# Half of the experts' weight loads issued through ScalarE's DMA queue

## The chip, the cores and the metric

The kernel runs on one core of one Trainium2 chip. The metric is device time in microseconds of one execution; lower is better. PE is TensorE, DVE is VectorE, ACT is ScalarE, POOL is GpSimd and SP is SyncE, the engine that here does nothing but wait and issue DMAs.

## The reference

Two transformer blocks in a row on one sequence of 256 tokens with 1024 channels, all in float32. The first has attention and an MLP; the second has an mLSTM branch, a differential attention branch and, last, a mixture of 16 experts in which each expert chooses its 32 tokens:

```python
def expert_choice_ffn(h, w_router, w_gate, w_up, w_down):
    aff = softmax(einsum('bsd,de->bse', h, w_router))
    g, idx = lax.top_k(aff.transpose(0, 2, 1), cap)          # cap = 32 tokens for each of 16 experts
    xe = h[bidx, idx]
    hid = silu(einsum('becd,edf->becf', xe, w_gate)) * einsum('becd,edf->becf', xe, w_up)
    ye = einsum('becf,efd->becd', hid, w_down) * g[..., None]
    return zeros_like(h).at[bidx, idx].add(ye)
# second block: x = x + expert_choice_ffn(rms_norm(x)); then a final rms_norm(x) * norm_f_g
```

Each expert has three matrices, gate and up of 1024 x 2048 and down of 2048 x 1024, 8 MB each. The experts' weights are 402.7 MB in all, and each byte is used once.

## The kernel before

The experts' stage is the second part of the program, from about 550 us on. The weights of an expert come in six **units** of 4 MB: unit u = 6e + kind, where kinds 0 and 1 are the two halves of the gate matrix of expert e, 2 and 3 those of the up matrix, 4 and 5 those of the down matrix. There are 96 units, 0 to 95. A unit is a load of 128 partitions by 32 KB, contiguous in memory for each partition. It goes into one of five buffers of `expert_ring`. Unit 5 has a place of its own, so that from unit 11 on, unit u takes the buffer that unit u - 5 has left.

PE works through the units in order, 32 matmuls each (L1255 for gate and up, L1294 for down), and counts `pairs_used` up twice in each unit, so that `pairs_used >= 2u + 2` says that unit u is used. Between kinds 3 and 4 of an expert DVE forms the product of silu and up (L1957), PE transposes it (L669) and DVE copies it back (L1963); after every fourth expert's kind 3 PE also gathers the tokens of the next four experts (L1199). After kind 5 ACT copies the expert's result `ye` and PE scatters it into the sum in PSUM (L1303).

Before the change all unit loads are issued by SP, in order, in one loop (L642). For each unit it waits until the unit that holds the buffer is used and then issues the DMA:

```python
if n >= BUFFERS:
    sp.wait_ge(pairs_used, 2 * unit_of(n - BUFFERS) + (1 if halved(u) else 2))
src = gate_up[kind // 2][e, kind % 2] if kind < 4 else down[e, kind - 4]
if not halved(u):
    sp.dma_start(expert_ring[:, FILL[b], :], src).then_inc(unit_loaded[b], 16)
    continue
```

A few units are loaded in pieces (`halved`): the first ones, 6 and 7, and the last, 95, which comes as 2 MB, 1 MB and two times 512 KB (L645, L649). PE waits on `unit_loaded` of the buffer before the first matmul of a unit.

ACT has three instructions for each expert: the silu after kind 1 (L2327), the copy `selx` of the scatter matrix (L2332, after kind 3), and the copy of `ye` after kind 5 (L2334). At expert 12 it also issues the load of the final gain row `gfinal`, 4 KB spread to 128 partitions (L2330), which is used only after the last expert. After the last expert come the final norm on ACT (L2338) and DVE (L1970) and the stores.

Of the kernel before, what the change touches and what calls it, by code (L numbers as in the profile page):

```python
# [37 lines left out]
P = 128  # L38
# [11 lines left out]
EXPERTS = 16  # L50
# [17 lines left out]
BUFFERS = 5  # L68
FILL = (3, 4, 0, 1, 2)
UNITS_EACH = 6  # L70
# [77 lines left out]
def build_program(nc, A, out, bias_scratch):  # L148
    with ExitStack() as ctx:
# [3 lines left out]
        def sems(text):  # L153
            return [ctx.enter_context(nc.semaphore(n)) for n in text.split()]
# [15 lines left out]
        expert_ring = nc.alloc_sbuf_tensor_at("expert_ring", [P, BUFFERS, UNIT], F32, offset=ring_at)  # L170
# [49 lines left out]
        def view(at, *shape):  # L220
# [79 lines left out]
        unit_loaded = [ctx.enter_context(nc.semaphore(f"unit_loaded{i}")) for i in range(BUFFERS)]  # L300
# [35 lines left out]
        pairs_used, selx_turned, selx_ready, silu_set, hid_set, hid_turned, hidT_set, ye_set, scattered_first, scattered = sems(  # L336
            "pairs_used selx_turned selx_ready silu_set hid_set hid_turned hidT_set ye_set scattered_first scattered")
# [31 lines left out]
        def used(g):  # L369

            if g == G_WOUT0:
                return g + 1 + N_ADA12
            return g + 1 - (G_ADA12 <= g < G_ADA12 + N_ADA12)
# [9 lines left out]
        def split_done(eng, g):  # L383

            eng.wait_ge(slot_split, 2 * (SPLIT.index(g) + 1))
# [28 lines left out]
        def fill_of(u):  # L414

            return u - (u > APART)

        def unit_of(n):

            return n + (n >= APART)  # L420

        def fills(u):

            return [unit_of(n) for n in range(fill_of(u) % BUFFERS, fill_of(u) + 1, BUFFERS)]
# [5 lines left out]
        def halved(u):  # L430

            return u in (1, 2, 3, APART + 1, APART + 2, EXPERTS * UNITS_EACH - 1)

        def second_of(u):

            return 16 * sum(2 if n in (1, 2) else 1 for n in fills(u) if halved(n))

        def everywhere(row, n):

            return bass.AP(row.tensor, row.offset, [[0, P], [1, n]])  # L440
# [84 lines left out]
        @block.sync  # L525
        def _(sp):
            sp.dma_start(xres[:, :, :], A["x"][0].rearrange("(t p) d -> p t d", p=P)).then_inc(x_in, 16)
            down = A["w_down_e_2"][0].rearrange("e (q p c) n -> e q p (c n)", q=2, p=P)
            gate_up = [A[n][0].rearrange("e (p h k) n -> e h p (k n)", p=P, h=2) for n in ("w_gate_e_2", "w_up_e_2")]

            def load_gain(which, k):

# [56 lines left out]
            for u in range(1, EXPERTS * UNITS_EACH):  # L589
                e, kind, n = u // UNITS_EACH, u % UNITS_EACH, fill_of(u)  # L590
                b = n % BUFFERS
                if u == 1:
                    def early(u, at, to, sem):

                        b = fill_of(u) % BUFFERS
                        kind = u % UNITS_EACH
                        sp.dma_start(expert_ring[:, FILL[b], at * SLOT:to * SLOT],
                                     gate_up[kind // 2][u // UNITS_EACH, kind % 2][:, at * SLOT:to * SLOT])\
                            .then_inc(sem[b], 16)

                    sp.wait_ge(unit_out, 2 * MH)
                    early(1, 0, 2, unit_loaded)
                    split_done(sp, G_UP + 3)
                    early(2, 0, 2, unit_loaded)
                    sp.wait_ge(mixed, 2)
                    early(1, 2, 3, second_loaded)
                    split_done(sp, G_WOUT2)
                    early(2, 2, 3, second_loaded)
                    sp.wait_ge(mixed, 4)
                    early(1, 3, 4, second_loaded)  # L610
                    sp.dma_start(ahead_y, down[0, 1][:, 4 * D:6 * D]).then_inc(ahead_loaded, 16)
                    split_done(sp, G_WOUT2 + 1)
                    early(2, 3, 4, second_loaded)
                    split_done(sp, G_WOUT2 + 2)
                    early(3, 0, 1, unit_loaded)
                    split_done(sp, G_WOUT2 + 3)
                    early(3, 1, 2, unit_loaded)
                    sp.wait_ge(slots_used, used(G_WOUT2 + 2))
                    early(3, 2, 4, second_loaded)
                    sp.wait_ge(slots_used, PRELUDE)  # L620
                if u <= 3:
                    continue
                if u == APART:
                    sp.wait_ge(logit16, 2)
                    sp.dma_start(ahead_x, down[0, 1][:, 6 * D:7 * D]).then_inc(ahead_x_loaded, 16)
                    continue
                if u == APART + 3:
                    sp.wait_ge(rank_cols, 1)
                    sp.dma_start(ahead_c, down[0, 1][:, 7 * D:8 * D]).then_inc(ahead_c_loaded, 16)
                if u == APART + 1:  # L630
                    sp.wait_ge(slots_used, PRELUDE + 1)
                    early(u, 0, 1, unit_loaded)
                    sp.wait_ge(pairs_used, 1)
                    early(u, 1, 2, unit_loaded)
                    sp.wait_ge(pairs_used, 2)
                    early(u, 2, 4, second_loaded)
                    continue
                if n >= BUFFERS:
                    sp.wait_ge(pairs_used, 2 * unit_of(n - BUFFERS) + (1 if halved(u) else 2))
                src = gate_up[kind // 2][e, kind % 2] if kind < 4 else down[e, kind - 4]  # L640
                if not halved(u):
                    sp.dma_start(expert_ring[:, FILL[b], :], src).then_inc(unit_loaded[b], 16)  # L642
                    continue
                if u == EXPERTS * UNITS_EACH - 1:
                    sp.dma_start(expert_ring[:, FILL[b], 0:4 * D], src[:, 0:4 * D]).then_inc(unit_loaded[b], 16)  # L645
                    sp.wait_ge(pairs_used, 2 * unit_of(n - BUFFERS) + 2)
                    for sem, first, last in zip(tail_loaded, (4, 6, 7), (6, 7, 8)):
                        part = slice(first * D, last * D)
                        sp.dma_start(expert_ring[:, FILL[b], part], src[:, part]).then_inc(sem, 16)  # L649
                    continue  # L650
                for half, sem in enumerate((unit_loaded[b], second_loaded[b])):
                    part = slice(half * UNIT // 2, (half + 1) * UNIT // 2)
                    if half == 1:
                        sp.wait_ge(pairs_used, 2 * unit_of(n - BUFFERS) + 2)
                    sp.dma_start(expert_ring[:, FILL[b], part], src[:, part]).then_inc(sem, 16)
            for t in range(NT):
                for half in range(2):
                    c = slice(512 * half, 512 * (half + 1))
# [1318 lines left out]
        def _(act):  # L1977
# [35 lines left out]
            def expect(function):  # L2013

                N.activation(foreseen[:, :], eps[:, :], function)
# [109 lines left out]
            for half in range(2):  # L2125
                for i in range(half * MLP_HALF, (half + 1) * MLP_HALF):
                    if g_w1(i) not in RAW:
                        act.wait_ge(slots_used, used(g_w1(i)))
                        for m in range(2):
                            c = A_B1 + 2 * i + m  # L2130
# [7 lines left out]
                    c = 2 * (i % MLP_HALF)  # L2138
# [24 lines left out]
            for i in range(N_MIX2):  # L2163
                if i < N_MIX2 - 1:
                    round_slot(act, G_MIX2 + i + 2)
                if i in range(4, 4 + 8):
                    c = i - 4
# [8 lines left out]
                if i < 4:  # L2176
                    dst, src = zpad[:, 2 * i:2 * i + 2, 2:2 + S], turned_
                elif i == 5:
                    dst, src = vo[:, 1, 0:MW], PS[:, i % 4, :]
                elif i < 10:  # L2180
                    dst, src = dqk[:, 2 * (i - 6):2 * (i - 6) + 2, :], turned_
                elif i == 11:
                    dst, src = dv[:, 1, :], PS[:, i % 4, :]
                else:
                    dst, src = vo[:, 1, MW:2 * MW], PS[:, i % 4, :]
# [39 lines left out]
            for u in range(2 * MH + 1):  # L2225
# [6 lines left out]
                if u == MH + 2:  # L2232
                    act.wait_ge(factors2_set, 1)
                    for t in range(NT):
                        for h in range(MH):
                            n, w = 8 * t + h, work[:, t, h * P:(h + 1) * P]
# [30 lines left out]
            for t in range(NT):  # L2267
                for u in range(MH, 2 * MH):
                    n, w = 8 * t + u, work[:, t, u * P:(u + 1) * P]
# [50 lines left out]
            normalise(1, slice(4, KD))  # L2320
            act.wait_ge(exp16, 1)
            expect(ACT.Silu)
            for e in range(EXPERTS):
                act.wait_ge(pairs_used, 2 * (UNITS_EACH * e + 2))
                if e == 0:
                    act.wait_ge(seeded, 2 * NT)
                N.activation(silu[:, :], PS[:, 0, :], ACT.Silu).then_inc(silu_set, 1)  # L2327
                if e == EXPERTS - GROUP:
                    act.wait_ge(gathered, 2 * EXPERTS // GROUP + 3)
                    act.dma_start(gfinal, everywhere(A["norm_f_g_2"], D)).then_inc(gfinal_in, 16)  # L2330
                act.wait_ge(selx_turned, e + 1)
                N.activation(selx[:, :], PS[:, 0, 0:S], ACT.Copy).then_inc(selx_ready, 1)  # L2332
                act.wait_ge(pairs_used, 2 * (UNITS_EACH * e + 6))
                N.activation(ye[:, :], PS[:, 3, :], ACT.Copy).then_inc(ye_set, 1)  # L2334
            expect(ACT.Sqrt)
# [86 lines left out]
```

## Time and profile before

| | us |
|---|---|
| median of 3 runs | 1452.87 (1452.32 to 1454.32) |
| the profiled execution | 1452.38 |
| its span | 1450.6 |
| PE busy | 1060.3 (73%) |
| DVE busy | 425.8 (29%) |
| ACT busy | 346.2 (24%) |
| POOL busy | 85.8 (6%) |

The span is what the hardware profiler saw from the first to the last instruction; the execution's own time is a little longer. Shares are of the span. The DMA queues moved 514.50 MB at a mean of 355 GB/s; q1 is SP's hardware queue, q10 is ACT's, q0 is POOL's, and q8 and q14 fetch instructions.

### The profile page before, as it was taken

How to read it: one execution, taken by the hardware profiler on the slowest of the kernel's cores; microseconds unless marked ns; L12 is line 12 of the kernel's file. 1: busy time of each engine (PE TensorE's matmuls, PEld its weight loads, DVE VectorE, ACT ScalarE, POOL GpSimd, SP SyncE). 2: the span in 40 equal slices, each digit the busy share in tenths (PEclk: the TensorE clock that was granted, in tenths of full speed). 3: DMA queues.
4: the chain of work that ended last, by engine and by line, in shares of the span. 5: the costliest groups of instructions: out<-in, count | busy, mean ns of one | idle time of the engine just before them, and what ended most of it. 6: DMA issues, size and time to landing. Idle time of an engine off the chain costs nothing.

```text
span 1450.6 us, 15820 instructions
## 1 busy us (share of the span) xinstructions
PE 1060.3 (73%) x6734; PEld 599.1 (41%) x6734; DVE 425.8 (29%) x767; ACT 346.2 (24%) x600; POOL 85.8 (6%) x60
## 2 busy tenths in 40 slices
PE   6999999999999999766665565565545565655655
PEld 3866888888989985211211111121111121111111
DVE  3577776756979863000000000000000000000001
ACT  3566654636555942000000000000000000000001
POOL 1420059000000000000000000000000000000000
PEclk9999999999999999988888887788788878788788
DMA  9996468554564689999999999999999999999996
GB/s 362 338 376 205 147 230 262 191 186 146 175 232 125 261 342 418 431 431 430 428 432 432 432 431 430 432 431 430 429 431 432 433 433 428 431 429 431 433 432 279
DMA packets 83144, 514.50 MB, mean 355 GB/s; under 512 B 6659, under 2 KB 49134, under 8 KB 67330
## 3 DMA queue, kind: packets, MB, share of 16 engines
q1 hardware_dynamic: 82360, 512.68, 87.4%
q8 instruction: 53, 0.87, 0.3%
q10 hardware_dynamic: 490, 0.61, 0.1%
q0 software_dynamic: 224, 0.20, 0.0%
q14 instruction: 17, 0.14, 0.0%
HBM read 512.27 MB, written 1.07 MB: 354 GB/s over the span
## 4 chain that ended last, share of the span: by engine, by line
DMA 56%; PE 33%; DVE 7%; ACT 2%; issue 1%; SPq 1%; POOL 0%; DVEq 0%; ACTq 0%
DMA expert_ring<-in_w_up_e 20%; DMA expert_ring<-in_w_gate_e 18%; DMA expert_ring<-in_w_down_e 15%; PE PS L1255 6%; PE PS L675 5%; PE PS L677 5%; PE PS L676 5%; PE PS L722 4%; PE PS L724 2%; DVE wR L403 2%; PE PS L1294 2%; DMA ring<-in_w_in 1%; PE PS L749 1%; DMA ring<-in_w_ada 1%; ACT wR L393 1%
## 5 line engine op out<-in xcount | busy, mean ns | idle before, releaser
L1255 PE MATMUL PS<-expert_ring,xeT 128*32 128x512 f32 x2048 | 309.7, 761 | 225.9 <-DMA expert_ring<-in_w_up_e 124.0
L1255 PEld LDWEIGHTS PS<-expert_ring,xeT 128*32 128x32 f32 x2048 | 74.3, 135 | 458.1 <-issue 207.7
L1957 DVE TENSOR_TENSOR expert_rows<-expert_rows,PS 128x512 f32<-128x512 f32 x16 | 11.0, 687 | 805.6 <-PE PS L1255 805.6
L1294 PE MATMUL PS<-expert_ring,expert_rows 128*32 128x512 f32 x992 | 155.4, 777 | 103.7 <-DMA expert_ring<-in_w_down_e 101.4
L403 DVE TENSOR_TENSOR wR<-ring,wR 128x1024 fp32r<-128x1024 f32 x144 | 177.8, 1276 | 55.3 <-ACT wR L393 55.0
L393 ACT ACTIVATE wR<-ring 128x1024 fp32r<-128x1024 f32 x144 | 144.5, 1053 | 112.0 <-PE PS L677 110.8
L1294 PEld LDWEIGHTS PS<-expert_ring,expert_rows 128*32 128x32 f32 x992 | 38.7, 137 | 208.9 <-issue 119.5
L722 PE MATMUL PS<-hR,wR 128*128 128x512 f32 x320 | 112.2, 396 | 1.7 <-DVE wR L403 1.6
L724 PE MATMUL PS<-hR,wR 128*128 128x256 f32 x320 | 89.1, 278 | 0.0
L2332 ACT ACTIVATE selx<-PS 128x256 f32<-128x256 f32 x16 | 6.1, 384 | 322.4 <-PE PS L669 322.4
L675 PE MATMUL PS<-hR,wR 128*128 128x256 f32 x280 | 80.2, 286 | 0.8 <-DVE wR L403 0.8
L677 PE MATMUL PS<-hR,wR 128*128 128x256 f32 x280 | 79.2, 283 | 0.0
L676 PE MATMUL PS<-hR,wR 128*128 128x256 f32 x280 | 79.2, 283 | 0.0
L2327 ACT ACTIVATE expert_rows<-PS 128x512 f32<-128x512 f32 x16 | 9.6, 597 | 283.7 <-PE PS L1255 283.7
L2334 ACT ACTIVATE expert_rows<-PS 128x512 f32<-128x512 f32 x16 | 9.6, 597 | 257.0 <-PE PS L1294 257.0
L722 PEld LDWEIGHTS PS<-hR,wR 128*128 128x128 f32 x320 | 60.0, 188 | 16.5 <-issue 2.4
L724 PEld LDWEIGHTS PS<-hR,wR 128*128 128x128 f32 x320 | 60.2, 188 | 0.1
L675 PE MATMUL PS<-wR,hR 128*128 128x512 f32 (+1 forms) x144 | 55.7, 386 | 1.7 <-DVE wR L403 1.4
L677 PE MATMUL PS<-wR,hR 128*128 128x512 f32 (+1 forms) x144 | 54.3, 377 | 0.0
L676 PE MATMUL PS<-wR,hR 128*128 128x512 f32 (+1 forms) x144 | 54.3, 377 | 0.0
L675 PEld LDWEIGHTS PS<-hR,wR 128*128 128x128 f32 x280 | 53.7, 192 | 1.1 <-issue 1.0
L676 PEld LDWEIGHTS PS<-hR,wR 128*128 128x128 f32 x280 | 53.7, 192 | 0.0
(317 smaller groups left out, 1281.9 us busy)
## 6 DMA issues: line engine op xcount, KB each, us to landing
expert_ring<-in_w_down_e SPq DMA_DIRECT2D x30, 4096.0 KB, 44.2
expert_ring<-in_w_up_e SPq DMA_DIRECT2D x30, 4096.0 KB, 43.1
expert_ring<-in_w_gate_e SPq DMA_DIRECT2D x29, 4096.0 KB, 43.2
ring<-in_w SPq DMA_DIRECT2D x32, 1024.0 KB, 6.1
ring<-in_w_in SPq DMA_DIRECT2D x31, 1024.0 KB, 5.7
ring<-in_w_ada SPq DMA_DIRECT2D x16, 1024.0 KB, 12.8
ring<-in_w_out SPq DMA_DIRECT2D x8, 1024.0 KB, 10.6
expert_ring<-in_w_gate_e SPq DMA_DIRECT2D x4, 2048.0 KB, 12.4
```

The lines of the kernel that those rows point to most:

```text
L393: nc.scalar.activation(halves(g, 0)[:, piece], slot(g)[:, piece], ACT.Copy).then_inc(slot_rounded, 1)
L403: by.tensor_tensor(halves(g, 1)[:, piece], slot(g)[:, piece], halves(g, 0)[:, piece], ALU.subtract)\
L675: nc.tensor.matmul(o, first[0], second[0], start=start, stop=False, skip_group_check=onto)
L676: nc.tensor.matmul(o, first[0], second[1], start=False, stop=False, skip_group_check=onto)
L677: return nc.tensor.matmul(o, first[1], second[0], start=False, stop=stop, skip_group_check=onto)
L722: nc.tensor.matmul(o.rearrange("p (a s) -> p a s", a=2), w[0][:, k, cols], hR[:, :, k, :], start=(k == 0), stop=False, skip_group_check=True)
L724: mm = nc.tensor.matmul(o[:, 0:S], w[1][:, k, cols], hR[:, 0, k, :], start=False, stop=(k == KD - 1), skip_group_check=True)
L749: mm = nc.tensor.matmul(PS[:, bank, m * S + t * P:m * S + (t + 1) * P], k8(g)[:, k, m * P:(m + 1) * P], hT[:, k, t * P:(t + 1) * P], start ...
L1255: mm = nc.tensor.matmul(PS[32 * j:32 * j + 32, kind // 2, :], xeT[:, e // GROUP % 2, k, own], w[:, j // 2, j % 2, :, :], start=(k == 0), s ...
L1294: mm = nc.tensor.matmul(PS[32 * at:32 * at + 32, 3, :], hidT[:, c % 4, 2 * q + c // 4, :], w[c][:, 512 * half:512 * (half + 1)], start=(q ...
L1957: V.tensor_tensor(hid[:, :], silu[:, :], PS[:, 1, :], ALU.mult).then_inc(hid_set, 1)
L2327: N.activation(silu[:, :], PS[:, 0, :], ACT.Silu).then_inc(silu_set, 1)
```

## The change

From unit 13 on, every odd unit but the last (13, 15, ... 93, 41 loads) is issued by ACT. SP skips these units. ACT waits for the use of unit u before it issues unit u + 5, and this is put at three places of its loop over the experts: ahead of the silu, ahead of the copy of selx and ahead of the copy of ye. Source, destination, size and semaphore of each load stay as they were, and so does the unit whose use it waits for.

```diff
+        def by_act(u):
+
+            return u > 2 * UNITS_EACH and u % 2 == 1 and u < EXPERTS * UNITS_EACH - 1
+
+        down = A["w_down_e_2"][0].rearrange("e (q p c) n -> e q p (c n)", q=2, p=P)
+        gate_up = [A[n][0].rearrange("e (p h k) n -> e h p (k n)", p=P, h=2) for n in ("w_gate_e_2", "w_up_e_2")]
+
+        def unit_source(u):
+
+            e, kind = u // UNITS_EACH, u % UNITS_EACH
+            return gate_up[kind // 2][e, kind % 2] if kind < 4 else down[e, kind - 4]
+
...
+                if by_act(u):
+                    continue
                 if n >= BUFFERS:
                     sp.wait_ge(pairs_used, 2 * unit_of(n - BUFFERS) + (1 if halved(u) else 2))
-                src = gate_up[kind // 2][e, kind % 2] if kind < 4 else down[e, kind - 4]
+                src = unit_source(u)
...
+
+            def load_behind(u):
+
+                if u + 5 < EXPERTS * UNITS_EACH and by_act(u + 5):
+                    act.wait_ge(pairs_used, 2 * u + 2)
+                    b = fill_of(u + 5) % BUFFERS
+                    act.dma_start(expert_ring[:, FILL[b], :], unit_source(u + 5)).then_inc(unit_loaded[b], 16)
+
             for e in range(EXPERTS):
+                load_behind(UNITS_EACH * e)
                 act.wait_ge(pairs_used, 2 * (UNITS_EACH * e + 2))
...
+                load_behind(UNITS_EACH * e + 2)
                 act.wait_ge(selx_turned, e + 1)
                 N.activation(selx[:, :], PS[:, 0, 0:S], ACT.Copy).then_inc(selx_ready, 1)
+                load_behind(UNITS_EACH * e + 4)
                 act.wait_ge(pairs_used, 2 * (UNITS_EACH * e + 6))
```

## Rows read from the trace of the kernel before

**Rows 1.** The page: its head, and the chain that ended last by engine.

```profile
span 1450.6 us, 15820 instructions
...
DMA 56%; PE 33%; DVE 7%; ACT 2%; issue 1%; SPq 1%; POOL 0%; DVEq 0%; ACTq 0%
```

**Rows 2.** Windows: stretch, us, busy by engine (instructions), PE clock, DMA share, GB/s.

```profile
650.00:700.00 50.00, 29.91 (x186) 8.18 (x182) 1.77 (x4) 0.98 (x2) 0.00 (x0) 0.81 1.01 433
...
1300.00:1400.00 100.00, 55.28 (x348) 15.11 (x348) 3.54 (x8) 2.56 (x5) 0.00 (x0) 0.84 1.00 430
```

**Rows 3.** Waits: engine and line, whom for, us in total, times, longest.

```profile
ACT selx L2332 <- PE PS L669: 322.4, 16, 24.8
ACT expert_rows L2327 <- PE PS L1255: 283.7, 16, 19.9
ACT expert_rows L2334 <- PE PS L1294: 257.0, 16, 19.8
...
SPq L642 <- PE PS L1255: 491.8, 53, 12.3
```

**Rows 4.** Timeline: start, length, instruction, count [idle before, releaser].

```profile
588.07 10.51 PE L1255 MATMUL PS<-expert_ring,xeT 128*32 128x512 f32 x96
...
599.07 3.64 PE L1255 MATMUL PS<-expert_ring,xeT 128*32 128x512 f32 x32 [0.49 <-DMA expert_ring<-in_w_up_e]
...
1223.92 5.49 PE L1255 MATMUL PS<-expert_ring,xeT 128*32 128x512 f32 x32 [6.08 <-DMA expert_ring<-in_w_gate_e]
1229.48 0.37 ACTq L2330 DMA_DIRECT2D ybuf<-in_norm_f_g  x1
1233.69 5.34 PE L1255 MATMUL PS<-expert_ring,xeT 128*32 128x512 f32 x32 [4.28 <-DMA expert_ring<-in_w_up_e]
1244.47 5.45 PE L1255 MATMUL PS<-expert_ring,xeT 128*32 128x512 f32 x32 [5.45 <-DMA expert_ring<-in_w_up_e]
1254.28 5.34 PE L1294 MATMUL PS<-expert_ring,expert_rows 128*32 128x512 f32 x32 [2.57 <-DMA expert_ring<-in_w_down_e]
1263.89 5.98 PE L1294 MATMUL PS<-expert_ring,expert_rows 128*32 128x512 f32 x32 [4.27 <-DMA expert_ring<-in_w_down_e]
...
1302.73 5.34 PE L1255 MATMUL PS<-expert_ring,xeT 128*32 128x512 f32 x32 [4.64 <-DMA expert_ring<-in_w_up_e]
```

**Rows 5.** DMA, 600 to 1400 us: queues (packets, MB, share of engines), issues (median us to landing).

```profile
q1 hardware_dynamic: 11806, 343.94, 100.0%
...
q10 hardware_dynamic: 144, 0.52, 0.2%
...
expert_ring<-in_w_up_e SPq DMA_DIRECT2D x28, 4096.0 KB, 43.1
```

**Rows 6.** DMA queues, 1229.5 to 1233.5 us, then 1233.5 to 1244.5.

```profile
q10 hardware_dynamic: 7, 0.03, 1.8%
...
q1 hardware_dynamic: 145, 4.23, 89.0%
q10 hardware_dynamic: 137, 0.50, 11.1%
```

**Rows 7.** Timeline of the end.

```profile
1376.04 0.33 SPq L642 DMA_DIRECT2D expert_ring<-in_w_up_e  x1
...
1420.82 6.02 PE L1255 MATMUL PS<-expert_ring,xeT 128*32 128x512 f32 x32 [4.37 <-DMA expert_ring<-in_w_up_e]
...
1428.44 0.69 DVE L1963 COPY expert_rows<-PS 128x512 f32<-128x512 f32 x1 [0.84 <-PE PS L669]
...
1430.62 3.64 PE L1294 MATMUL PS<-expert_ring,expert_rows 128*32 128x512 f32 x32 [2.00 <-DMA expert_ring<-in_w_down_e]
...
1440.37 1.05 PE L1294 MATMUL PS<-expert_ring,expert_rows 128*32 128x512 f32 x4 [0.18 <-DMA expert_ring<-in_w_down_e]
1441.47 0.60 ACT L2334 ACTIVATE expert_rows<-PS 128x512 f32<-128x512 f32 x1 [12.42 <-PE PS L1294]
```

**Rows 8.** Timeline of a gather and the unit behind it.

```profile
1191.08 3.84 PE L1199 MATMUL PS<-sel,work 128*128 128x128 f32 x32
...
1197.24 3.64 PE L1294 MATMUL PS<-expert_ring,expert_rows 128*32 128x512 f32 x32 [0.56 <-DVE expert_rows L1963]
```

More of the change, by code:

```diff
@@ L527, in _ @@
             sp.dma_start(xres[:, :, :], A["x"][0].rearrange("(t p) d -> p t d", p=P)).then_inc(x_in, 16)
-            down = A["w_down_e_2"][0].rearrange("e (q p c) n -> e q p (c n)", q=2, p=P)
-            gate_up = [A[n][0].rearrange("e (p h k) n -> e h p (k n)", p=P, h=2) for n in ("w_gate_e_2", "w_up_e_2")]
             def load_gain(which, k):
```

## The prediction

> **What bounds the kernel now.** I read the page's head and its chain of work first [rows 1]. The profiled execution took 1452.38 us, 1.78 more than its span. DMA is the largest share of the chain (56%), nearly all of it the experts' weights. The windows by stage [rows 2] say where: from 650 to 1400 us the DMA engines' busy share is 1.00 or 1.01 at 430 to 433 GB/s, while PE is busy 55 to 61 us of each 100. PE sits idle before its units until one lands [rows 4]. So the experts' stage is set by bytes over rate and ends when the last unit has landed; what follows is a short tail. In the waits [rows 3] SP, too, waits for little but used buffers, and ACT waits some twenty us before each instruction of this stage.
>
> Landings come 9.71 us apart: unit 77 is taken up at 1263.89 and unit 81 at 1302.73, four loads in 38.84 [rows 4]. Between 600 and 1400 us q1 moved 343.94 MB in 11806 packets [rows 5]. That is 82.0 loads of 4.194 MB and 144 packets a load, 9 for each of 16 engines. The 128 rows of 32 KB give 8 large ones each, and the ninth is small. 9.71 / 8 = 1.21 us per large packet. Five buffers, each refilled as soon as it is used, keep 4.4 loads outstanding (43.1 us to landing over 9.71).
>
> **The change, part by part.** 41 loads (units 13, 15, ... 93) leave SP's queue. On SP that removes 41 issues of 0.33 us [rows 7], hidden there: over four loads were queued in front of each. On ACT it adds 41 waits and 41 issues, which I price at the 0.37 us of ACT's own DMA issue in this stage [rows 4], 15 us in all. Behind them on ACT stand the silu, the copy of selx and the copy of ye. Each of these waits for a unit after the one that the load ahead of it waits for, at least 3.6 us later, so an issue is over when they are released. The cover is ACT's idle time before those three (284, 322 and 257 us [rows 3]); without it 15 us would be the cost. I take 0. Each moved load waits for the same unit's use as before.
>
> *The rate with two queues.* No stretch has two streams of large packets. The nearest is gfinal, 512 KB on ACT's queue (q10) beside SP's loads. Between 1233.5 and 1244.5 us q10 moved 137 packets and q1 145 [rows 6]: one for one, whatever their size. From unit 73 to 77, with gfinal between them, the landings took 39.97 us [rows 4]; four loads alone take 38.84, so gfinal cost 1.13 us, where 0.52 MB at 431 GB/s would be 1.22. From 73 to 76 (30.36 less 3 x 9.71) it cost 1.23, from 74 to 75 (10.78 less 9.71) 1.07. So 16 changes of queue on each engine cost between -0.15 and +0.01 us. In the new kernel some 85 loads of 8 packets alternate, 680 changes: -6.4 to +0.4 us. I take 0, since the engines' busy share leaves nothing that a second queue could fill.
>
> The Trainium skill (DMA: Bandwidth & Descriptors, "Issuing engines are not separate DMA queues") speaks against any gain: DMAs of all issuing engines run on the same 16 and interleave, so spreading them saves only issue time. By it alone the sum would be 0 and the time 1452.9; on the rate, the rows of gfinal agree. It says nothing of what the interleaving does to the order of landing, which is worked out next from rows.
>
> *The order of landing.* While both queues hold work each load takes 16 turns, 2 x 9.71 = 19.4 us, and an odd and an even one are under way together. PE then meets two units at once: about 5.9 us for the first after a long idle (5.49 and 6.02 [rows 4, 7]), 3.64 for the second. From issue to first packets I take 4 us, as gfinal's (issued 1229.48 [rows 4], 7 of its 144 packets before 1233.5 [rows 6]). Units 6 to 8 end at 598.6 and 9 is there at 599.1 [rows 4]. So 13 is issued at 598.6, starts at 602.6 and lands at 622, before its turn. Beside it 10 has 3 packets at 1.21 us and 5 at 2.43: it lands at 615, 11 at 631. 15, issued when 10 is used (620.7), runs from 624.7 to 644; 17 is not issued until 12 is used, near 653.5, and starts at 657.5. In that gap SP's queue has all engines and catches up: 14 lands at 657, then 16 and 17 both near 677. From there on ACT's next load is ready in time (even landing + 5.9 + 4 is less than 19.4), and units 2k and 2k + 1 land within a us or two of each other. The DMA engines never run dry: a pair costs PE 5.9 + 3.64, plus 2.4 for the transposes and 3.8 more where a gather falls in [rows 7, 8], under 16 of 19.4 us. So the last byte lands when it did.
>
> Then expert 12: gfinal now stands in ACT's queue behind unit 77. It takes 8 turns with 4 KB packets, while SP's queue takes 8 turns with 32 KB, a whole load. From there the odd loads are one place later: 79 lands with 80, not with 78, and so on to 93 with 94. That is the step that costs. At the end now, 93 is taken up at 1420.82, 94 at 1430.62, the last piece of 95 at 1440.37, and PE ends 1.05 later [rows 7]. If 93 lands X us before the last piece, PE still has to do after it: 6.0 (unit 93) + 2.4 (product, transposes, copy: 1426.84 to 1429.2) + 3.64 (unit 94) + 3.64 (unit 95, all there by then) = 15.7 us; the last two at full clock, as the unit behind a gather ran (3.64 after 0.56 idle [rows 8]). The end moves by 15.7 - X - 1.05 where that is positive. 93 landing exactly with 94 gives X = 9.75 and +4.9. One us earlier gives X = 10.3 (what remains of 94 then gets all engines) and +4.35. I take that. Bounds: 93 some 10 us ahead of 94 gives X = 14.7 and 0; 93 five us behind 94, while 95 runs beside it, gives X = 7.3 and +7.4.
>
> Sum: issues 0, rate 0, tail +4.35, the epilogue (from 1441.47 on [rows 7]) unchanged. The profiled execution would take 1456.7, and the median of the runs, now 0.5 above it, 1457.2.
>
> **Rivals.**
> *No change (1452.9, up to 1455).* The odd loads keep a lead of 5 us or more over their even partners. If a load's first packet comes 1.5 us after its issue and PE's first unit of a pair is short, 17 and 19 start sooner, the lead outlives gfinal, and 93 lands 14 us or more before the end. For it: bytes and rate. Against: gfinal's 4 us and the eight turns lost to it.
> *A larger loss (1461 to 1468).* Two interleaved streams of large packets cost the engines something that gfinal, one 4 KB row read 128 times, could not show: 1% of 850 us is 8.5, to 1461. Or ACT's queue is served less than one for one: then 93 would land last, X near 0, +14.6, 1467.5. Against both: 145 to 137, and -0.15 to +0.01.
> *Faster (1446.5 to 1450).* If each of 680 changes of queue gives back the 0.009 us of the lower bound, -6.4 with a tail of 0 gives 1446.5; beside a tail of 4.35 it would have to be more than 7.3 to be told from no change. Against: a busy share of 1.00 already, and landings that repeat to 0.1 us.
> *That the change does nothing* is excluded: ACT's DMAs have a queue of their own, q10, beside SP's q1 [rows 5].
>
> **How the numbers follow.** 0.2% is 2.9 us, about what these runs can tell from no change. Tail as forecast (+0 to +7.4, likeliest +4.35): 0.55, of which 0.08 lies under +2.9. No change: 0.28. Larger loss: 0.11. Faster: 0.06. So slower 0.47 + 0.11 = 0.58, same 0.08 + 0.28 = 0.36, faster 0.06. The range leaves out most of the larger loss and of the faster case, and holds the others: 1451.0 to 1461.5; the forecast's own is 1453 to 1460.
>
> **What would show it.** Right: a DMA share of 1.00 and 430 to 433 GB/s in the same windows; q10 with about 172 MB; odd and even units landing together every 19.4 us and PE in bursts of two; odd loads one place later after gfinal; unit 93 within 12 us of the last piece of 95, and PE without a wait for that piece. Wrong: 93 landing 15 us or more before the end (no tail), fewer GB/s (two streams cost something), stretches with a DMA share under 1.00 before 1430 us (starved engines), or PE waiting for ACT.

## The result, and the profile after

The changed kernel takes 1457.98 us (median of 5 runs, 1457.05 to 1459.0) against 1452.71 for the kernel before beside it (1451.88 to 1454.32): a ratio of 1.0038, 95% interval 1.0026 to 1.0049. Run once more (e8 below) it gave 1.0028, 1.0017 to 1.0040. The profiled execution took 1457.91 us, with a span of 1456.1. Three executions, one of the kernel before and one each of e2 and e3 below, took 1647.58 to 3781.58 us and are left out of all ratios; e2's was its profiled one, so e5 is the same kernel again, for its trace.

First the windows of the changed kernel, with the columns of [rows 2]:

```profile
650.00:700.00 50.00, 27.28 (x214) 8.05 (x210) 1.77 (x4) 1.58 (x3) 0.00 (x0) 0.84 1.01 433
...
1300.00:1400.00 100.00, 53.86 (x362) 14.24 (x352) 3.54 (x8) 3.15 (x6) 0.00 (x0) 0.76 1.00 429
1400.00:1440.00 40.00, 21.15 (x142) 5.39 (x142) 1.38 (x2) 0.98 (x2) 0.00 (x0) 0.79 0.93 395
1440.00:1446.00 6.00, 6.00 (x60) 1.81 (x59) 0.00 (x0) 0.00 (x0) 0.00 (x0) 1.00 0.03 14
```

The DMA engines are as full as before and move the same GB/s. What is new is the last row: from 1440 to 1446 us next to nothing is left to load (14 GB/s), and PE is busy all six us. In the kernel before PE ended 1.05 us after it took up the last piece.

The DMA queues of the changed kernel from 600 to 1400 us, as in [rows 5]:

```profile
q1 hardware_dynamic: 6102, 177.93, 51.7%
q10 hardware_dynamic: 5833, 166.50, 48.4%
...
expert_ring<-in_w_gate_e ACTq DMA_DIRECT2D x14, 4096.0 KB, 32.5
expert_ring<-in_w_up_e SPq DMA_DIRECT2D x14, 4096.0 KB, 49.5
...
ybuf<-in_norm_f_g ACTq DMA_DIRECT2D x1, 512.0 KB, 39.4
```

The two queues share the bytes about evenly. Where every load took 43 to 45 us from issue to landing, ACT's now take some 32 and SP's some 49. Over the whole execution q10 moved 172.58 MB. gfinal takes 39.4 instead of 15.1, since it waits for ACT's loads ahead of it.

Then PE's timeline in the changed kernel (L1267 and L1306 are L1255 and L1294 of before), as in [rows 4, 7]. A row of x64 is two units without a wait between them; where the product and its transposes lie between the two units of a pair, as between 81 and 82, they are two rows:

```profile
589.32 10.51 PE L1267 MATMUL PS<-expert_ring,xeT 128*32 128x512 f32 x96
600.44 3.64 PE L1267 MATMUL PS<-expert_ring,xeT 128*32 128x512 f32 x32 [0.62 <-DMA expert_ring<-in_w_up_e]
...
617.53 5.39 PE L1306 MATMUL PS<-expert_ring,expert_rows 128*32 128x512 f32 x32 [11.67 <-DMA expert_ring<-in_w_down_e]
633.23 6.07 PE L1306 MATMUL PS<-expert_ring,expert_rows 128*32 128x512 f32 x32 [10.31 <-DMA expert_ring<-in_w_down_e]
...
649.01 8.44 PE L1267 MATMUL PS<-expert_ring,xeT 128*32 128x512 f32 x64 [6.91 <-DMA expert_ring<-in_w_gate_e]
659.95 7.08 PE L1267 MATMUL PS<-expert_ring,xeT 128*32 128x512 f32 x64 [2.49 <-DMA expert_ring<-in_w_up_e]
...
679.46 8.58 PE L1306 MATMUL PS<-expert_ring,expert_rows 128*32 128x512 f32 x64 [10.66 <-DMA expert_ring<-in_w_down_e]
...
1264.25 9.72 PE L1306 MATMUL PS<-expert_ring,expert_rows 128*32 128x512 f32 x64 [7.94 <-DMA expert_ring<-in_w_down_e]
...
1276.69 3.64 PE L1267 MATMUL PS<-expert_ring,xeT 128*32 128x512 f32 x32
1295.53 9.45 PE L1267 MATMUL PS<-expert_ring,xeT 128*32 128x512 f32 x64 [15.19 <-DMA expert_ring<-in_w_gate_e]
1314.96 6.54 PE L1267 MATMUL PS<-expert_ring,xeT 128*32 128x512 f32 x32 [9.98 <-DMA expert_ring<-in_w_up_e]
...
1430.93 6.58 PE L1267 MATMUL PS<-expert_ring,xeT 128*32 128x512 f32 x32 [9.64 <-DMA expert_ring<-in_w_up_e]
...
1439.86 7.07 PE L1306 MATMUL PS<-expert_ring,expert_rows 128*32 128x512 f32 x64 [0.56 <-DVE expert_rows L1975]
```

Read it by units. 10 and 11 come late, 16 us apart. 12 and 13 are done together at 649.01, 16 and 17 at 679.46, and so on in pairs of an even unit with the odd one above it, up to 76 with 77 at 1264.25. Then 78 is done alone (1276.69), and PE waits 15.19 us for 79, which is done with 80 (1295.53). From there each pair is odd first (81, with 82 behind the transposes, at 1314.96), and 93 starts at 1430.93. Behind it PE never waits for a weight again: 94 and 95 are one row of 64 matmuls, released by DVE's copy, not by a load.

The start of the experts' stage differs between executions, here by 1.25 us. So I also measure from the start of unit 6 (588.07 and 589.32) to PE's end of unit 95 (1440.37 + 1.05 = 1441.42, and 1439.86 + 7.07 = 1446.93): 853.35 us before, 857.61 after, +4.26.

### The profile page after: what moved, and what is told of

Its sections match the earlier page's. It is cut to its first block, busy times and chain, and to the rows that moved or that the text cites. A ratio compares the mean times of both kernels' runs of the same rounds, so it can differ in the third digit from the quotient of the medians.

```text
span 1456.1 us, 15820 instructions
## 1 busy us (share of the span) xinstructions
PE 1023.5 (70%) x6734; PEld 595.0 (41%) x6734; DVE 425.5 (29%) x767; ACT 346.1 (24%) x600; POOL 86.0 (6%) x60
## 3 DMA queue, kind: packets, MB, share of 16 engines
q10 hardware_dynamic: 6394, 172.58, 27.6%
## 4 chain that ended last, share of the span: by engine, by line
DMA 47%; PE 39%; DVE 7%; ACT 2%; another core or an unknown queue 2%; issue 2%; SPq 1%; POOL 0%; DVEq 0%; ACTq 0%
DMA expert_ring<-in_w_up_e 30%; DMA expert_ring<-in_w_down_e 13%; PE PS L1267 8%; PE PS L687 5%; PE PS L689 5%; PE PS L688 5%; PE PS L734 4%; PE PS L1306 4%; DMA expert_ring<-in_w_gate_e 3%; PE PS L736 2%; DVE wR L403 2%; DMA ring<-in_w_ada 2%; PE PS L681 1%; SPq L564 1%
## 5 line engine op out<-in xcount | busy, mean ns | idle before, releaser
L1267 PE MATMUL PS<-expert_ring,xeT 128*32 128x512 f32 x2048 | 288.2, 724 | 247.6 <-DMA expert_ring<-in_w_up_e 132.5
L1267 PEld LDWEIGHTS PS<-expert_ring,xeT 128*32 128x32 f32 x2048 | 71.3, 130 | 460.5 <-issue 212.4
L1306 PE MATMUL PS<-expert_ring,expert_rows 128*32 128x512 f32 x992 | 139.4, 722 | 124.1 <-DMA expert_ring<-in_w_down_e 121.8
L1306 PEld LDWEIGHTS PS<-expert_ring,expert_rows 128*32 128x32 f32 x992 | 37.3, 130 | 215.5 <-issue 185.3
```

Source lines behind the costliest of these rows:

```text
L1267: mm = nc.tensor.matmul(PS[32 * j:32 * j + 32, kind // 2, :], xeT[:, e // GROUP % 2, k, own], w[:, j // 2, j % 2, :, :], start=(k == 0), s ...
L1306: mm = nc.tensor.matmul(PS[32 * at:32 * at + 32, 3, :], hidT[:, c % 4, 2 * q + c // 4, :], w[c][:, 512 * half:512 * (half + 1)], start=(q ...
```

## The experiments

Three explanations had to be told apart. **Order of landing**: gfinal's packets cost ACT's queue eight turns (a turn is one packet of one queue on one DMA engine), so the odd loads fall one place back, 93 lands with 94, and PE is left with 93, 94 and 95 behind the last loads. **Pairs**: that units land two at a time costs by itself, through PE's bursts. **Two queues**: their alternation or ACT's issues cost rate. All times are ratios to the kernel before, run beside each; "stage" is the stretch defined above.

| | ratio, 95% interval | stage, us | against before |
|---|---|---|---|
| before | 1 | 853.35 | |
| changed kernel | 1.0038, 1.0026 to 1.0049 | 857.61 | +4.26 |
| e1, gfinal on SP | 0.9997, 0.9988 to 1.0005 | 853.34 | -0.01 |
| e2 and e5, unit 93 on SP | 1.0000, 0.9991 to 1.0009 (e2) | 853.21 (e5) | -0.14 |
| e3, quarter of gfinal | 1.0019, 1.0009 to 1.0028 | 855.55 | +2.20 |
| e4, even units on ACT | 1.0028, 1.0017 to 1.0039 | 858.53 | +5.18 |
| e6, odd units from 79 | 1.0003, 0.9993 to 1.0012 | 853.29 | -0.06 |
| e7, gfinal in four | 1.0036, 1.0022 to 1.0050 | 858.48 | +5.13 |
| e8, changed kernel again | 1.0028, 1.0017 to 1.0040 | 857.77 | +4.42 |

**e1, gfinal on SP's queue.** All 41 loads stay on ACT.

```diff
+                if u == 78:
+                    sp.wait_ge(pairs_used, 2 * (UNITS_EACH * 12 + 2))
+                    sp.wait_ge(gathered, 2 * EXPERTS // GROUP + 3)
+                    sp.dma_start(gfinal, everywhere(A["norm_f_g_2"], D)).then_inc(gfinal_in, 16)
...
-                if e == EXPERTS - GROUP:
-                    act.wait_ge(gathered, 2 * EXPERTS // GROUP + 3)
-                    act.dma_start(gfinal, everywhere(A["norm_f_g_2"], D)).then_inc(gfinal_in, 16)
```

> The changed kernel, with the load of gfinal issued by SP ahead of unit 78 instead of by ACT behind unit 77. Order-of-landing theory: ACT's queue no longer loses eight turns, so the odd loads stay beside the even load one below them; 93 lands with 92, about 19 us before the last piece of 95, PE waits for that piece again, and the time is that of the kernel before, 1452.7, within 2 us. Rival, pairs cost by themselves (bursts of PE at a lower clock, whichever pairs they are): the loss of about 5 us stays, 1458. Rival, two queues or ACT's issues cost rate: it stays too, and shows as fewer GB/s before 1430 us.

Median 1451.91 us of 11 runs; before 1452.5. The whole loss is gone. Its timeline on PE, around gfinal and at the end:

```profile
1265.36 9.19 PE L1310 MATMUL PS<-expert_ring,expert_rows 128*32 128x512 f32 x64 [9.01 <-DMA expert_ring<-in_w_down_e]
...
1294.43 16.88 PE L1271 MATMUL PS<-expert_ring,xeT 128*32 128x512 f32 x128 [17.08 <-DMA expert_ring<-in_w_gate_e]
...
1402.73 8.78 PE L1271 MATMUL PS<-expert_ring,xeT 128*32 128x512 f32 x64 [6.67 <-DMA expert_ring<-in_w_gate_e]
1422.15 9.30 PE L1271 MATMUL PS<-expert_ring,xeT 128*32 128x512 f32 x64 [10.65 <-DMA expert_ring<-in_w_up_e]
...
1433.81 6.47 PE L1310 MATMUL PS<-expert_ring,expert_rows 128*32 128x512 f32 x56 [0.57 <-DVE expert_rows L1979]
1440.46 1.05 PE L1310 MATMUL PS<-expert_ring,expert_rows 128*32 128x512 f32 x4 [0.18 <-DMA expert_ring<-in_w_down_e]
1441.69 1.05 PE L1310 MATMUL PS<-expert_ring,expert_rows 128*32 128x512 f32 x4 [0.18 <-DMA expert_ring<-in_w_down_e]
```

92 and 93 are one row at 1422.15, and the last two pieces are each waited for again. Pairs and two queues are here in full, with 167.68 MB on q10 between 600 and 1400 us, and cost nothing: both rivals fall.

One thing I had not expected: gfinal held up SP's queue here. 78 is taken up 29.07 us after 76 (1265.36 to 1294.43), not 19.4, and 78 to 81 are one row of 128 matmuls. But this place was won back: from 1295 to 1300 us q10 moved nothing and q1 ran at a share of 1.01, and behind it the pairs are even with odd again, down to 92 with 93. So a place lost to gfinal does not always stay lost; it did in ACT's queue.

**e2 and e5, unit 93 on SP's queue.** gfinal stays on ACT.

```diff
-            return u > 2 * UNITS_EACH and u % 2 == 1 and u < EXPERTS * UNITS_EACH - 1
+            return u > 2 * UNITS_EACH and u % 2 == 1 and u < EXPERTS * UNITS_EACH - 3
```

> The changed kernel, with unit 93 given back to SP (ACT has 13 to 91); gfinal stays on ACT. Order-of-landing theory: odd loads still fall one place back at expert 12, and 91 lands with 92, but from there SP's queue holds 93, 94 and 95 in order with all engines to itself; 93 lands about 19 us before the last piece, no backlog, 1452.7 within 2 us. Both rivals (cost of pairs, cost of two queues): 40 of 41 moved loads are still moved, so at least 4.5 of the 5 us stay, 1457.5 or more.

> The same kernel as e2_unit93_on_sync, for its trace. Order-of-landing theory: 79 lands with 80 and 91 with 92 as in the changed kernel (odd loads one place back), then 93 alone about 19 us and 94 about 10 us before the last piece of 95, and PE waits for that piece. Rival, that giving 93 back undid the shift itself: 91 lands with 90.

e2: median 1453.06 of 11 runs, ratio 1.0000. One load of 41 carries the loss. e5, a single execution of 1454.28 us, shows how, in PE's timeline:

```profile
1276.92 3.64 PE L1267 MATMUL PS<-expert_ring,xeT 128*32 128x512 f32 x32 [0.67 <-DMA expert_ring<-in_w_gate_e]
1296.25 9.88 PE L1267 MATMUL PS<-expert_ring,xeT 128*32 128x512 f32 x64 [15.69 <-DMA expert_ring<-in_w_gate_e]
...
1413.17 13.19 PE L1267 MATMUL PS<-expert_ring,xeT 128*32 128x512 f32 x96 [7.56 <-DMA expert_ring<-in_w_gate_e]
...
1432.52 10.80 PE L1306 MATMUL PS<-expert_ring,expert_rows 128*32 128x512 f32 x64 [4.38 <-DMA expert_ring<-in_w_down_e]
```

The shift at 79 is there as in the changed kernel. But 91, 92 and 93 are one row of 96 matmuls ending at 1426.36, and PE waits 4.38 us for 94. The wait for the last piece of 95 that I expected is not there: 94 and 95 are one row, 10.80 us long at a granted clock that was 0.50 from 1432 to 1438 us, yet it ends in time. So the shift costs nothing until it meets the end.

**e3, a quarter of gfinal.** Only 256 of the gain row's 1024 columns are loaded, so the output's other columns are scaled by what lay there.

```diff
-                    act.dma_start(gfinal, everywhere(A["norm_f_g_2"], D)).then_inc(gfinal_in, 16)
+                    act.dma_start(gfinal[:, 0:D // 4], everywhere(A["norm_f_g_2"], D // 4)).then_inc(gfinal_in, 16)
```

> The changed kernel, with gfinal loaded for its first 256 of 1024 columns only (three quarters of the final gain row are left unloaded, so the final scaling reads other values there): 1 KB rows in place of 4 KB, 128 of them as before. Theory that turns are lost, one for each packet whatever its size: eight turns as before, odd loads one place back from 79 on, 93 within 12 us of the last piece, 1457 (0.9 us less than now for the 0.39 MB not moved). Theory that what counts is the bytes or the time of the transfer in ACT's queue: the shift is a quarter, the odd loads keep near the even load below them, 93 lands 17 us or more before the last piece and the loss is gone, 1452 to 1453.

Median 1455.8, 1.2 us under what I expected, but clear of no change. PE's timeline:

```profile
1276.23 3.64 PE L1267 MATMUL PS<-expert_ring,xeT 128*32 128x512 f32 x32
1293.85 8.42 PE L1267 MATMUL PS<-expert_ring,xeT 128*32 128x512 f32 x64 [13.97 <-DMA expert_ring<-in_w_gate_e]
...
1429.26 5.55 PE L1267 MATMUL PS<-expert_ring,xeT 128*32 128x512 f32 x32 [9.00 <-DMA expert_ring<-in_w_up_e]
```

The shift is whole: 78 alone, 79 with 80. With a quarter of the bytes it would have been a quarter if bytes or time counted; the number of packets was unchanged. The stage is 2.06 us shorter than the changed kernel's. 1.03 of it is unit 93 itself (5.55 for 6.58 us), 1.03 its earlier start (840.58 for 841.61 us from the start of unit 6), for which the missing bytes would give 0.9 by my estimate. The first part does not come of the edit: e8, with all of gfinal, has unit 93 at 5.42 us.

**e4, the even units on ACT**, the odd ones on SP, and gfinal on SP.

```diff
-            return u > 2 * UNITS_EACH and u % 2 == 1 and u < EXPERTS * UNITS_EACH - 1
+            return u > 2 * UNITS_EACH and u % 2 == 0 and u < EXPERTS * UNITS_EACH - 1
...
-                load_behind(UNITS_EACH * e)
...
+                load_behind(UNITS_EACH * e + 1)
...
-                load_behind(UNITS_EACH * e + 2)
+                load_behind(UNITS_EACH * e + 3)
...
-                load_behind(UNITS_EACH * e + 4)
+                load_behind(UNITS_EACH * e + 5)
```

> The mirror of the change: the even units 14 to 94 on ACT (issued behind the use of the odd units), the odd ones on SP, and gfinal on SP ahead of unit 79. Order-of-landing theory: without any turn lost the pairs are 13 with 14, 15 with 16, up to 93 with 94, since ACT's load lands with the SP load one below it; so the tail comes back with no part of gfinal: 93 within 12 us of the last piece, +4 to +6 over before, 1457 to 1459. Theory that gfinal's place in ACT's queue costs in some other way than by the pairing: 1452.7 within 2.

Median 1456.63. The loss is back with gfinal out of ACT's queue. By its edit alone this run does not separate the parity from gfinal, since gfinal stands again in the queue of the odd units. PE's and SP's timelines do, with the end behind them:

```profile
1234.42 9.42 PE L1271 MATMUL PS<-expert_ring,xeT 128*32 128x512 f32 x64 [7.45 <-DMA expert_ring<-in_w_gate_e]
1240.46 0.33 SPq L651 DMA_DIRECT2D ybuf<-in_norm_f_g  x1
...
1303.55 8.99 PE L1271 MATMUL PS<-expert_ring,xeT 128*32 128x512 f32 x64 [18.23 <-DMA expert_ring<-in_w_gate_e]
...
1431.51 6.42 PE L1271 MATMUL PS<-expert_ring,xeT 128*32 128x512 f32 x32 [9.49 <-DMA expert_ring<-in_w_up_e]
...
1440.29 7.07 PE L1310 MATMUL PS<-expert_ring,expert_rows 128*32 128x512 f32 x64 [0.56 <-DVE expert_rows L1979]
```

73 and 74 are a pair, odd first, before gfinal is issued; 79 comes late (gfinal is ahead of it in SP's queue), but with 80, so the pairs are the same behind gfinal as ahead of it. The parity makes them, without gfinal. The end is the picture of the changed kernel: 93 late, and 94 and 95 one row behind it.

**e6, the odd units from 79 on.** ACT issues eight loads, and gfinal comes ahead of them.

```diff
-            return u > 2 * UNITS_EACH and u % 2 == 1 and u < EXPERTS * UNITS_EACH - 1
+            return u > 13 * UNITS_EACH and u % 2 == 1 and u < EXPERTS * UNITS_EACH - 1
```

> The change made for the odd units from 79 to 93 only (8 loads); gfinal stays on ACT, where it is now ahead of all of ACT's unit loads. Order-of-landing theory: gfinal's eight turns are over before unit 79 stands in the queue or cost it at most a short wait, 79 gets ahead as unit 13 did, the pairs settle as 2k with 2k + 1 within some units, 93 lands with 92, about 19 us before the last piece: 1452.5 within 2 us. Theory that any odd load on ACT next to gfinal or at the end costs: +4 to +5, 1457.

Median 1452.12, ratio 1.0003. At the end PE's timeline has 92 and 93 as one row:

```profile
1420.83 10.05 PE L1267 MATMUL PS<-expert_ring,xeT 128*32 128x512 f32 x64 [9.90 <-DMA expert_ring<-in_w_up_e]
```

So neither gfinal on ACT nor unit 93 on ACT costs anything alone. With the odd units on ACT, it takes gfinal among ACT's loads.

**e7, gfinal in four transfers** of 256 columns at the same place: the same bytes, four times the packets.

```diff
-                    act.dma_start(gfinal, everywhere(A["norm_f_g_2"], D)).then_inc(gfinal_in, 16)
+                    for c in range(0, D, D // 4):
+                        row = A["norm_f_g_2"]
+                        part = bass.AP(row.tensor, row.offset + c, [[0, P], [1, D // 4]])
+                        act.dma_start(gfinal[:, c:c + D // 4], part).then_inc(gfinal_in, 16)
...
-            dve.wait_ge(gfinal_in, 16)
+            dve.wait_ge(gfinal_in, 16 * 4)
```

> The changed kernel, with gfinal loaded by ACT in four transfers of 256 columns, so the same bytes in four times the packets (32 for each engine in place of 8), at the same place. Turn theory: while ACT's queue spends 32 turns on small packets, SP's queue sends out all it has (some 20 packets for each engine), so 79 lands some 30 us after 78, not 20 as in the changed kernel; PE and SP then wait for 79, and the pairs settle again as 79 with 80 and so on (SP cannot run further ahead than its buffers), so the end is as in the changed kernel: 1457 to 1460. Byte theory: 79 comes 20 us after 78 as in the changed kernel.

PE's timeline around 79:

```profile
1275.99 3.64 PE L1267 MATMUL PS<-expert_ring,xeT 128*32 128x512 f32 x32
1303.50 8.59 PE L1267 MATMUL PS<-expert_ring,xeT 128*32 128x512 f32 x64 [23.87 <-DMA expert_ring<-in_w_gate_e]
```

and its windows while PE waits there:

```profile
1280.00:1290.00 10.00, 0.00 (x0) 0.00 (x0) 0.00 (x0) 0.00 (x0) 0.00 (x0) 0.64 1.01 429
1290.00:1300.00 10.00, 0.00 (x0) 0.00 (x0) 0.00 (x0) 0.00 (x0) 0.00 (x0) 0.50 1.00 431
```

79 starts 714.87 us after unit 6, where the changed kernel has 706.21 and 706.96 (e8): some 8 us later for the same bytes. From 78 to 79 it is 27.5 us (30 expected), where the changed kernel has 18.8 and 20.3 (e8). A cost for each transfer, four in place of one, would fit that too, but the queues from 1265 to 1285 us show the turns:

```profile
q1 hardware_dynamic: 284, 8.26, 95.9%
q10 hardware_dynamic: 284, 0.26, 3.8%
```

Packet for packet, with 8.26 MB for one queue and 0.26 MB for the other. Turns are what is lost. Even a wait of 23.87 us costs nothing there that these runs can tell, since the DMA engines stay full. The pairs then settle as in the changed kernel, and so does the time (1457.52).

**e8, the changed kernel again.**

> The changed kernel itself, once more, beside the other one on the same chip: 1.003 to 1.0045 of the kernel before by either theory. It gives the spread of the start of the experts' stage, 1.25 us later in the changed kernel's trace than in that of before: if the change caused that, its trace shows it again and the loss is 5.3 us; if not, the loss is the tail's, 4.2.

Median 1456.79 of 6 runs. Its PE timeline:

```profile
586.11 10.51 PE L1267 MATMUL PS<-expert_ring,xeT 128*32 128x512 f32 x96
...
1429.03 5.42 PE L1267 MATMUL PS<-expert_ring,xeT 128*32 128x512 f32 x32 [9.10 <-DMA expert_ring<-in_w_up_e]
```

Here the stage starts 1.96 us earlier than in the kernel before, not 1.25 later, so the start belongs to the execution and not to the change. From unit 6 on the loss is 4.42 us.

## Why the prediction was right, point by point

- **ACT's issues, 0 us.** Right. e1 has all 41 at a ratio of 0.9997.
- **The rate, 0 us (bounds -6.4 to +0.4).** Right. 431 GB/s and a DMA share of 1.00 with two full streams, and e1 again bounds it: its interval, -1.7 to +0.7 us, holds everything the two queues can do.
- **How the pairs form.** Predicted for 10, 11, 12, 14 and 16: 615, 631, 648, 657 and 677; with the 1.25 us of the later start the trace has them at 617.5, 633.2, 649.0, 659.95 and 679.5, so they come between 0.2 us before and 1.7 us after the forecast. The 4 us from issue to first packets, which went into these, is in the trace: ACT issues unit 13's load at 599.89, q10 moves nothing before 603.3, and 11 packets of it start in the next us.
- **gfinal moves the odd loads one place back.** Right: 79 with 80. That it is the number of turns, not bytes, rested on 137 against 145 packets before; e3 (fewer bytes, same shift) and e7 (same bytes, larger shift, 284 packets against 284) show it. That the place stays lost down to 93 I took without a reason: it held here, but e1 won its place back.
- **The tail, +4.35 us.** The trace has +4.26, and +4.42 in e8. By its terms, measured from the start of unit 6: the last byte came when it did before (the DMA share is 0.00 from 851.9 us on before, from 852.2 or sooner after), the last piece was taken up at 852.30 before, and 93 at 841.61, so X is 10.7 (10.3 predicted). Behind it came 6.58 + 2.35 + 7.07 = 16.0 us (15.7 predicted). In e8 93 was taken up at 842.92, so X is 9.4, and 14.85 us came behind it. So each term moves by a us between executions of the same kernel, in these two the same way, and their difference hardly did: that the sum hit within 0.1 us is in part luck. The runs' 1.0038 is 5.5 us and e8's 1.0028 is 4.1; 4.35 (1.0030) lies in both intervals.
- **The rivals.** No change: e1, e2 and e6 have its time, so it was close, one 512 KB transfer or one unit away. A larger loss from two streams or from an unevenly served queue: refuted by the rate and by e1. Faster: refuted by the same.

The time (1457.98) lies 0.8 us from the forecast of 1457.2; against the kernel before beside it the runs have +5.3 us, where +4.35 was forecast. What I did not foresee is PE's clock: in the pairs PE idles longer at a stretch, and the mean granted clock from 1300 to 1400 us fell from 0.84 to 0.76. It cost nothing while loads were the bound: e1 has 0.77 there and no loss. At the end unit 93 took 6.58 us where I took 6.02 from before, at a granted clock of 0.50 until 1436 us; but it took 5.42 in e8, so that is no steady price of the change.

## What to carry to other kernels

Where the DMA engines are already full, a second queue brings no bandwidth, but it changes the order in which loads land. Ask what the consumer still has to do after the last byte, and keep the last loads on one queue in the order of their use: one load of 41 carried the whole loss here. And count a small transfer in a busy queue by its packets: eight small ones on each engine held up their queue by a whole 4 MB load. Whether the queue wins that place back is another matter: it did in e1, where ACT had no load under way for a while, and not in the changed kernel. Why the two differ stays open.

## What the runs showed of the hardware that was not expected

- Two queues with 32 KB packets take turns at no cost that these runs can tell: 431 GB/s at a share of 1.00, and a ratio of 0.9997 (0.9988 to 1.0005) in e1.
- A pairing of loads, once formed, stays for tens of loads (16 with 17 up to 76 with 77, 79 with 80 up to 93 with 94), and it was the same after e7's larger disturbance. In e1 it was the same, 92 with 93, after gfinal had held up SP's queue.
- The last loads end on half of the engines only. In the kernel before the DMA share is 0.50 and 0.51 from 1434 to 1438 us, in the changed kernel 0.48 and 0.40 from 1436 to 1440; the packet records of the kernel before have 8 or 9 packets under way at a time from 1434.5 to 1438, where 16 or more were until 1433. Why some engines are several us behind the others at the end was not looked into.
